# State-space products of a hybrid block: 64-row and 64-column neighbours in alternating halves of TensorE's array, Toeplitz products in one run before the wait for the scan

## The reference, cut to what matters

```
bu = einsum("sbgh,gph->sbgp", u, b_bar)        # 32 groups, 16 inputs, 64 complex states each
state[s] = a_bar * state[s-1] + bu[s]          # over 1024 tokens
y = real(einsum("sbgp,ghp->sbgh", state, c_mat))
```

## Time and profile before

| | |
|---|---|
| time, median of three runs | 2245.61 us (2242.71 to 2249.5) |
| span of the profiled execution, the only time it left | 2245.3 us |
| TensorE matmul busy (PE) | 2197.2 us, 98% |
| TensorE weight load busy (PEld) | 1808.5 us, 81% |
| DVE busy | 1182.0 us, 53% |
| POOL busy | 1146.3 us, 51% |
| ACT busy | 586.7 us, 26% |
| DMA, mean | 87 GB/s |

### The profile page before, as it was taken

The page is one execution under the profiler, slowest core; times in us unless marked ns, Lnnn a source line. Parts: engine busy times, 40 slices in busy tenths (PEclk is TensorE's granted clock), DMA queues, the critical chain, the costliest instruction groups (busy, mean ns, idle before and its releaser), DMA issues.

```text
span 2245.3 us, 28196 instructions
## 1 busy us (share of the span) xinstructions
PE 2197.2 (98%) x9890; PEld 1808.5 (81%) x9890; DVE 1182.0 (53%) x1548; ACT 586.7 (26%) x887; POOL 1146.3 (51%) x828
## 2 busy tenths in 40 slices
PE   6999999999999999999999989999999999999998
PEld 4788888888888787888888878887888888888887
DVE  6854455453635898385674664336743333324246
ACT  4622232313133510000101121113522322223234
POOL 1564564737373443444444476553854646465560
PEclk8999999999999998999999999999999999999999
DMA  7132325241413531322222244421111121211111
GB/s 282 57 113 91 116 66 159 63 143 56 149 57 63 145 99 47 94 80 85 85 80 89 56 160 145 141 70 38 38 57 57 39 75 37 65 47 60 34 57 76
DMA packets 234354, 194.75 MB, mean 87 GB/s; under 512 B 22996, under 2 KB 207456, under 8 KB 233120
## 3 DMA queue, kind: packets, MB, share of 16 engines
q1 hardware_dynamic: 210624, 154.52, 22.5%
q10 hardware_dynamic: 23648, 39.20, 5.5%
HBM read 167.34 MB, written 25.17 MB: 86 GB/s over the span
## 4 chain that ended last, share of the span: by engine, by line
PE 87%; DVE 8%; ACT 1%; SPq 1%; POOL 1%; issue 1%; DMA 1%; ACTq 0%; DVEq 0%; POOLq 0%
PE unit_b L815 11%; PE unit_a L815 11%; PE unit_d L1161 10%; PE unit_b L1161 10%; PE unit_c L955 9%; PE unit_d L955 9%; PE unit_c L1161 7%; PE unit_a L1161 7%; PE unit_d L815 2%; PE unit_c L815 2%; DVE sc_b L2317 1%; PE unit_d L1292 1%; PE unit_c L1181 1%; DVE sc_a L2317 1%; PE unit_d L1181 1%; DVE tmp L2182 1%
## 5 line engine op out<-in xcount | busy, mean ns | idle before, releaser
L704 POOL TENSOR_TENSOR w_high<-raw,ones 128x512 fp32r<-128x512 f32 x136 | 190.1, 1398 | 421.5 <-PE unit_b L815 184.1
L743 POOL TENSOR_TENSOR w_low<-raw,w_high 128x512 fp32r<-128x512 f32 x200 | 273.4, 1367 | 209.3 <-ACT w_high L1476 193.6
L713 POOL TENSOR_TENSOR w_low<-raw,w_high 128x512 fp32r<-128x512 f32 x96 | 140.1, 1461 | 286.9 <-ACT w_high L1433 286.9
L1476 ACT ACTIVATE w_high<-raw 128x512 fp32r<-128x512 f32 x200 | 126.5, 632 | 402.6 <-PE unit_b L1161 141.8
L706 POOL TENSOR_TENSOR w_low<-raw,w_high 128x512 fp32r<-128x512 f32 x136 | 193.5, 1423 | 10.7
L743 POOL TENSOR_TENSOR w_low<-w_mixed,w_high 128x512 fp32r<-128x512 f32 x80 | 107.3, 1341 | 67.0 <-ACT w_high L1476 61.8
L2044 DVE TENSOR_TENSOR fg_two<-fg_one,unit_b 128x512 f32<-128x512 f32 x60 | 41.3, 688 | 170.5 <-PE unit_b L1161 170.4
L815 PE MATMUL unit_a<-h_high,w_high 128*128 128x512 f32 x400 | 123.6, 390 | 0.5 <-ACT u_all L1615 0.5
L815 PE MATMUL unit_b<-h_high,w_high 128*128 128x512 f32 x400 | 124.1, 392 | 0.0
L815 PE MATMUL unit_b<-h_low,w_high 128*128 128x512 f32 x400 | 123.6, 390 | 0.0
L815 PE MATMUL unit_b<-h_high,w_low 128*128 128x512 f32 x400 | 123.4, 390 | 0.0
(11 more groups left out here) (434 smaller groups left out, 5463.4 us busy)
## 6 DMA issues: line engine op xcount, KB each, us to landing
raw<-in_w_a SPq DMA_DIRECT2D x66, 512.0 KB, 4.5
raw<-in_w_b SPq DMA_DIRECT2D x66, 512.0 KB, 3.9
raw<-in_w_in SPq DMA_DIRECT2D x44, 512.0 KB, 3.8
ada_ring<-in_w_ada SPq DMA_DIRECT2D x84, 256.0 KB, 3.6
ada_first<-in_w_ada SPq DMA_DIRECT2D x8, 1024.0 KB, 14.0
sg_kept<-s ACTq DMA_DIRECT2D x16, 512.0 KB, 2.6
s<-sg_kept ACTq DMA_DIRECT2D x16, 512.0 KB, 3.4
ada_ring_last<-in_w_ada SPq DMA_DIRECT2D x28, 256.0 KB, 3.6
```

The source lines that it names most:

```text
L704: pool.tensor_tensor(high, raw[:, r, rows, :], one, ALU.mult).then_inc(high_split, 1)
L713: pool.tensor_tensor(low_, plain, high.bitcast(F32), ALU.subtract).then_inc(f.operand_low, 1)
L743: pool.tensor_tensor(low_, weight_plain(PRODUCTS[q][0], slots), high.bitcast(F32), ALU.subtract).then_inc(f.operand_low, 1)
L1476: act.activation(operand((RING[n] + q) % 4)[0], weight_plain(PRODUCTS[q][0], slots), ACT.Copy).then_inc(f.operand_high, 1)
```

## The change

Two loops are reordered, one is taken apart, and a wait is moved. The loops of lines 1267 and 1277 had `g2` outermost; it is now innermost, so consecutive products use the two halves of the array in turn. The loop of lines 1290 and 1292 becomes two: all 8 Toeplitz products first, behind the waits for `toep_loaded` and `unit_free[D_]`, and then, behind the wait for `scan_done`, the 16 products with 64 rows, again with `g2` innermost. The count, shapes and operands of the products are unchanged. The first Toeplitz product of each bank carries `start=True`, the others of the bank `start=False`.

```diff
-                for g2 in range(2):
-                    rows = slice(NS * g2, NS * g2 + NS)
-                    for kk in range(4):
-                        col = (4 * g2 + kk) * P
-                        for part in range(2):
+                for kk in range(4):
+                    for part in range(2):
+                        for g2 in range(2):
+                            rows = slice(NS * g2, NS * g2 + NS)
+                            col = (4 * g2 + kk) * P
                             last = pe.matmul(unit[D_][0:H, col:col + P], b_now[rows, kk, part, :],
...
-                for g2 in range(2):
-                    for kk in range(4):
-                        for part in range(2):
-                            col = (2 * kk + part) * P
+                for kk in range(4):
+                    for part in range(2):
+                        col = (2 * kk + part) * P
+                        for g2 in range(2):
                             last = pe.matmul(unit[C_][NS * g2:NS * g2 + NS, col:col + P],
...
-                pe.wait_ge(scan_done, t + 1)
                 pe.wait_ge(toep_loaded, 128 * (t + 1))
                 take(D_, here.unit[D_] + 2 * t + 1)
-                for g2 in range(2):
-                    rows = slice(NS * g2, NS * g2 + NS)
-                    for kk in range(4):
-                        dst = unit[D_][:, (4 * g2 + kk) * P:(4 * g2 + kk + 1) * P]
-                        pe.matmul(dst, toep[:, 4 * g2 + kk, :], u_chunk[:, 2 * kk + g2, :], start=True, stop=False)
-                        for part in range(2):
-                            last = pe.matmul(dst, ca[rows, kk, part, 1:9, :].rearrange("p d h -> p (d h)"),
-                                             sc_b[rows, kk, part, PAD:], start=False, stop=(part == 1))
+
+                def group(g2, kk):
+                    return unit[D_][:, (4 * g2 + kk) * P:(4 * g2 + kk + 1) * P]
+
+                for kk in range(4):
+                    for g2 in range(2):
+                        pe.matmul(group(g2, kk), toep[:, 4 * g2 + kk, :], u_chunk[:, 2 * kk + g2, :], start=(kk == 0),
+                                  stop=False, skip_group_check=True)
+                pe.wait_ge(scan_done, t + 1)
+                for kk in range(4):
+                    for part in range(2):
+                        for g2 in range(2):
+                            rows = slice(NS * g2, NS * g2 + NS)
+                            last = pe.matmul(group(g2, kk), ca[rows, kk, part, 1:9, :].rearrange("p d h -> p (d h)"),
+                                             sc_b[rows, kk, part, PAD:], start=False, stop=(part == 1),
+                                             skip_group_check=True)
                 last.then_inc(ssm_full, 1)
```

## The result

The changed kernel takes 2208.23 us (median of four runs, 2206.99 to 2210.3) where the kernel before takes 2245.32 (four runs): a ratio of 0.9831, 95% interval 0.9817 to 0.9845. That is 37.1 us faster. The forecast was 2222.3 with a range of 2211 to 2230.

The account below looks back on a forecast made before the run. TensorE, in flight for 98% of the span, was taken to bound the kernel. Gains of 16.05 us in turns 1 to 3 and 7.2 in turn 0 summed to 23.25, giving 2222.3 us, range 2211 to 2230.

Parts of the forecast that it names:

- Lines 1267 and 1277: Small-product blocks with halves in turn: loads and products overlap throughout, gaining 1.2 and 1.35 us a turn.
- The limit by `xt`: Line 1277 needs ACT's copy to `xt`, so it can't start before 955.34; line 1267 gains 1.2 us.
- The Toeplitz run: Mixed block of lines 1290 and 1292: 14 fewer changes of shape at 0.2 us, 2.8 us less a turn.
- Line 1292, 0 us: 64-row products with halves in turn: weight loads limit them, 3.5 us in either order, so no gain.
- Loads share one port: Line 1292: a second weight load begins when the first has streamed in; 128-column loads come 0.11 us apart.
- Rival (a): Line 1292: loads of different row halves run side by side, 1.75 us more a turn, 2214 us; chance 0.28.
- (c): Turn 0: the clock stays up, gaining 12.2 us there in place of 7.2, 2217.3 us; chance 0.07.
- DVE sets the scan's end here: Turn 0: the scan ends at 881.74 regardless, so TensorE's 2.55 us gain ahead becomes only longer wait.
- TensorE stands still for about 4 us: Turn 0, ahead of the 64-row products: the clock falls to 0.50 and they take 7.3 us.
- Nothing given back: Turns 1 to 3 and later waits: no new wait for the scan; the 5.67 us POOL wait only moves.

Follow-up runs that it names:

- e5: Changed kernel with DVE clearing the pad of `sc_b` four more times ahead of the scan in turn 0; 2211.99 us.
- e1: Changed kernel with the 16 products of 64 rows taking all of one half first, then all of the other; 2214.95 us.
- e6: Changed kernel with 64 moving columns instead of 128 in the 16 products of 64 rows; 2207.73 us, one execution.
- e11: Changed kernel with POOL's low halves of the slabs' weights made for only 32 of 128 columns; 2198.04 us, one execution.
- e8: Changed kernel with 64 moving columns instead of 128 in the products of line 1267; 2206.73 us, one execution.
- e9: Changed kernel with ACT instead of DVE clearing the two front pads of the scan's buffers, ahead of their use; 2207.17 us.
- e10: Changed kernel run once more without any edit, as a control; 2207.78 us.
- e7: Changed kernel with the 64-row products on 64 moving columns and all of one half first; 2217.05 us, one execution.
- e2: Changed kernel with all three kinds of small products one half after the other, keeping the Toeplitz run ahead of the wait; 2230.38 us.

## Why the prediction missed

- **Lines 1267 and 1277, 2.55 us a turn: right.** 2.52 measured alone. The limit by `xt` was right as well (2.03 us to the next block in turn 1). The overlap read at one change of half held for the whole block. The Trainium skill's rule that loads overlap matmuls in flight only across row groups ("TensorE: Matmul & The Clock Gate", Part 3, Packing small matmuls) doesn't hold for line 1277, whose halves are of columns: its 32 records take 1.97 us where they took 3.33.
- **The Toeplitz run, 2.8 us a turn: right.** 3.05 measured, the excess being the overlap at the change of half in line 1292, which the old order had broken up.
- **Line 1292, 0 us: the first step that failed.** "Loads share one port. Loads of 128 columns then fill that port as it is." They don't share it across row halves. I had read the stagger of loads in the earlier trace rows (0.05 us at 64 columns, 0.02 at 16) as one waiting for the other; it may be no more than the order in which they are issued. The size: 5.35 forecast against 7.00 a turn, 5 us in three turns, and 7.3 - 3.8 = 3.5 us in turn 0 even at the slow clock (3.78 in `e5`). Rival (a) had this price, 2214, with a chance of 0.28; the range, from 2211, left no room for it together with (c) or a shorter scan. The Trainium skill's sentence that different tiles load and multiply in parallel ("TensorEngine Tiling (Array Packing)", Key Properties) agrees with `e1` and `e6`.
- **Turn 0, "DVE sets the scan's end here": the second step that failed.** The start of the scan was fixed, its length was not. In the earlier trace rows the last four scan operations take 3.24 us, and in the earlier trace rows 3.27, where the same operations without POOL beside them take 1.13 (`e11`). POOL's splits follow TensorE, so the scan's end does too: 2.6 us. The Trainium skill has the rule that I had not weighed ("GPSIMD Engine Reference", 1. Specifications): POOL shares its SBUF interfaces with DVE and contends with DVE instructions that have two SBUF inputs, as each operation of this scan has. The trace agrees, with 41.4 against 51.3 us in `e11`.
- **"TensorE stands still for about 4 us", so the clock falls: followed from the second, and perhaps from the first.** The wait was 1.75 us, and the products behind it alternated. I priced the fall at once for the block and the slab; its absence is worth 1.8 + 1.5 us. That was rival (c), argued against by waits of 2.32 and 3.47 us that weren't the wait to come.
- **Nothing given back: right.** TensorE waits for the scan in no later turn, and the wait at the split after the turns is 5.6 us as it was.

The sum: 5 + 3.5 us of overlap of halves, 2.6 of the scan, 3.3 of the clock, less 0.9 of a later start are the 13.5 us by which the span's gain exceeds the forecast's 23.25.

What isn't settled is what decides on the clock behind a wait of 1.7 to 1.95 us. It stayed at 1.00 in all five profiled executions in which the alternating block followed (the changed kernel, `e6`, `e8`, `e9`, `e10`) and fell in two of the three in which one half came first (`e1` and `e7`, not `e2`). So the length of the wait alone doesn't decide it; that the order does is not shown. That POOL's operations delay DVE's is shown; no run here shows through which shared part they do.

## What to carry to other kernels

Where two products use different halves of TensorE's array, put them next to each other: their loads overlap, and by the estimate above their matmuls too; it was worth 1.4 us per 32 records here even where the load binds. A change of shape between products cost 0.2 us, so collect equal shapes, and put what doesn't need the awaited result ahead of the wait. Before an end on another engine is called fixed, look at what lengthens its operations: whatever follows the engine you speed up may move across it.

## What I had not expected of the hardware

- The same four scan operations of DVE take 1.13 us alone and 3.2 us beside a pair of POOL's 1.3 us operations. Ten pairs or nine beside a scan are 53.9 or 51.3 us.
- Behind one and the same wait of 1.95 us the granted clock fell to 0.50 in `e1` and `e7` and stayed at 1.00 in `e6` and `e8`; in turn 1 of `e7` it fell where TensorE had not waited. In `e1` the fall cost some 4.8 us.
- A small float32 product can be issued far faster than its usual 0.11 us a record: 0.027 us, halves in turn, with 16 weight columns and 64 moving ones.
